# Products over token chunks of 458, 458 and 254 columns, with one 508-column matmul for the high and low parts of the last chunk

## What is computed

```python
D_MODEL, D_FF, CONV_W = 1024, 2816, 3

def conv_ffn(x, left, g, w_gate, w_up, cw, cb, w_down):
    xn = rms_norm(x, g)
    a = xn @ w_gate
    L = x.shape[1]
    ap = jnp.concatenate([left.astype(a.dtype), a], axis=1)
    ac = cb + sum(ap[:, j:j + L] * cw[j] for j in range(CONV_W))
    y = (jax.nn.gelu(ac) * (xn @ w_up)) @ w_down
    return y, ap[:, -(CONV_W - 1):]

# in each of the two layers: x = x + attention(rms_norm(x) @ w_in) @ w_o; x = x + conv_ffn(x, ...)
```

## Time and profile before

| | us |
|---|---|
| median of 3 runs | 3441.87 |
| lowest, highest | 3436.18, 3450.18 |
| the profiled execution | 3446.24 |
| its span from first to last instruction | 3444.3 |
| PE busy in it | 3284.8 |
| DVE, ACT, POOL busy | 1624.4, 781.4, 881.8 |

### The profile page before, as it was taken

One profiled execution on the slowest core, in us unless ns is written; L12 is line 12 of the kernel. 1 busy time (PEld: TensorE's weight loads), 2 busy tenths in 40 slices (PEclk: granted clock), 3 DMA queues, 4 the chain that ended last, 5 costly groups with the idle time before them and its releaser, 6 DMA issues.

```text
span 3444.3 us, 49534 instructions
## 1 busy us (share of the span) xinstructions
PE 3284.8 (95%) x17911; PEld 3017.1 (88%) x17911; DVE 1624.4 (47%) x3150; ACT 781.4 (23%) x1867; POOL 881.8 (26%) x943
## 2 busy tenths in 40 slices
PE   8979999999999999999985999999999999999998
PEld 7957778899999999987684777777989999999997
DVE  4033442454444454454697355544244444444445
ACT  3043553100000000032454335443210000000001
POOL 3211222322222222231132133221232222222321
PEclk9955999999999999999996569999999999999998
DMA  3520000111111111122111000000211111111111
GB/s 106 82 75 1 1 2 19 37 37 43 37 43 43 37 42 37 39 83 50 23 48 46 21 1 1 1 1 1 76 36 44 43 37 43 43 37 37 43 43 64
DMA packets 179634, 129.18 MB, mean 38 GB/s; under 512 B 30961, under 2 KB 169649, under 8 KB 179270
## 3 DMA queue, kind: packets, MB, share of 16 engines
q1 hardware_dynamic: 179490, 127.32, 12.9%
HBM read 111.62 MB, written 15.16 MB: 37 GB/s over the span
## 4 chain that ended last, share of the span: by engine, by line
PE 88%; DVE 6%; issue 4%; ACT 1%; SPq 1%; DMA 0%; DVEq 0%; POOL 0%; POOLq 0%; ACTq 0%
PE ps_gemm L1235 30%; PE ps_gemm L1251 16%; PE ps_gemm L1201 14%; PE ps_out L1583 7%; PE ps_out L1417 5%; PE ps_tr L1301 4%; PE ps_far L1563 2%; PE ps_far L1465 2%; PE ps_near L1565 2%; PE ps_far L1397 1%; PE ps_tr L1287 1%; DVE xl L1821 1%; DVE pta L1816 1%; DVE m L2049 1%; DVE pt_b L1816 1%
## 5 line engine op out<-in xcount | busy, mean ns | idle before, releaser
L569 DVE TENSOR_TENSOR h<-h,ps_gemm 128x1170 f32<-128x1170 f32 x192 | 263.7, 1373 | 409.1 <-PE ps_gemm L1251 231.5
L1235 PE MATMUL ps_gemm<-xh,w_hi 128*128 128x390 f32 x1920 | 448.1, 341 | 0.0
L1235 PE MATMUL ps_gemm<-xh,w_lo 128*128 128x390 f32 x1920 | 448.1, 342 | 0.0
L1235 PE MATMUL ps_gemm<-xl,w_hi 128*128 128x390 f32 x1920 | 446.1, 340 | 0.0
L1077 POOL CAST w_hi<-w_raw 128x1024 fp32r<-128x1024 f32 x120 | 125.1, 1042 | 1129.1 <-PE ps_gemm L1235 623.8
L1235 PEld LDWEIGHTS ps_gemm<-xh,w_hi 128*128 128x128 f32 x1920 | 352.5, 189 | 0.0
L1235 PEld LDWEIGHTS ps_gemm<-xl,w_hi 128*128 128x128 f32 x1920 | 349.4, 189 | 0.0
L1235 PEld LDWEIGHTS ps_gemm<-xh,w_lo 128*128 128x128 f32 x1920 | 349.1, 189 | 0.0
L1080 POOL TENSOR_TENSOR w_lo<-w_raw,w_hi 128x1024 fp32r<-128x1024 f32 x120 | 288.2, 2402 | 18.5 <-POOL w_hi L1077 2.5
L1201 PE MATMUL ps_gemm<-xl,w_hi 128*128 128x390 f32 (+1 forms) x1152 | 275.3, 348 | 0.0
L1251 PE MATMUL ps_gemm<-gu_hi,w_hi 128*128 128x390 f32 x1056 | 247.4, 342 | 1.0 <-DVE h L569 1.0
(11 more groups left out here) (287 smaller groups left out, 5304.4 us busy)
## 6 DMA issues: line engine op xcount, KB each, us to landing
w_raw<-in_w_gate SPq DMA_DIRECT2D x44, 512.0 KB, 3.8
w_raw<-in_w_up SPq DMA_DIRECT2D x44, 512.0 KB, 3.8
w_raw<-in_w_down SPq DMA_DIRECT2D x44, 512.0 KB, 3.2
w_raw<-in_w_in_b SPq DMA_DIRECT2D x13, 512.0 KB, 4.3
w_raw<-in_w_qkv_a SPq DMA_DIRECT2D x10, 512.0 KB, 3.9
residual_park<-h SPq DMA_DIRECT2D x1, 4680.0 KB, 13.7
h<-residual_park SPq DMA_DIRECT2D x8, 585.0 KB, 8.7
out<-yt SPq DMA_DIRECT2D x9, 512.0 KB
```

Source lines behind the costliest of these rows:

```text
L569: dve.tensor_tensor(c3(h[:, m, :]), c3(h[:, m, :]), pse(j), ALU.add).then_inc(evac[j % 2], 1)
L1235: mm = pe.matmul(ps[j % 2][:, m_, 0:CH], w[:, k, :], x[:, k, m_ * CH:(m_ + 1) * CH], start=(k == 0 and w is wh and x is XH), stop=(k == KT ...
```

## The change

The chunks become 458, 458 and 254 columns (CH = 458, WL = 254). XH and XL become two halves of one tensor XX, gu_hi and gu_lo two halves of GU. In the FFN (`split=True`) the product of a high weight block with the third chunk of the high part and that of the low part become one matmul over 2 x 254 = 508 columns, which leaves the high part's sum in columns 0 to 253 of the third bank and the low part's in columns 254 to 507; so a block has eight matmuls there. VectorE adds the two halves: `tail_copy` copies the second half to a tile, `tail_of` adds the first half to it, and the consumer reads the tile. Outside the FFN (`split=False`) a block keeps nine matmuls, three of them of 254 columns. All takers of PSUM now use one instruction for the two chunks of 458 and one for the last chunk. The RMS scale is computed over the new chunks.

```diff
-CH = T // NCH
+CH = 458
+CHUNKS = ((0, CH), (CH, 2 * CH), (2 * CH, T))
+WL = T - 2 * CH
...
+        def bank_pair(j, r=slice(0, P)):
+
+            return ps[j % 2][r, 0:2, 0:CH]
+
+        def bank_last(j, r=slice(0, P)):
+
+            return ps[j % 2][r, 2, 0:WL]
+
+        def bank_rest(j, r=slice(0, P)):
+
+            return ps[j % 2][r, 2, WL:2 * WL]
...
+        def tail_copy(dve, j):
+
+            dve.tensor_copy(tail[j % 2][:], bank_rest(j)).then_inc(tail_in, 1)
+
+        def tail_of(dve, j, i=None):
+
+            wait_at(dve, tail_in, 2 * tail_no(j) + 1, 24, i)
+            dve.tensor_tensor(tail[j % 2][:], bank_last(j), tail[j % 2][:], ALU.add).then_inc(tail_in, 1)
+            wait_at(dve, tail_in, 2 * tail_no(j) + 2, 24, i)
+            return tail[j % 2][:]
...
-        def residual(dve, j, m, i=None):
+        def residual(dve, j, m, i=None, merged=True):
 
             wait_at(dve, mm_done, j + 1, 12, i)
-            dve.tensor_tensor(c3(h[:, m, :]), c3(h[:, m, :]), pse(j), ALU.add).then_inc(evac[j % 2], 1)
+            src = bank_last(j)
+            if merged:
+                tail_copy(dve, j)
+            dve.tensor_tensor(cols_pair(h[:, m, :]), cols_pair(h[:, m, :]), bank_pair(j), ALU.add)
+            if merged:
+                src = tail_of(dve, j, i)
+            dve.tensor_tensor(cols_last(h[:, m, :]), cols_last(h[:, m, :]), src, ALU.add).then_inc(evac[j % 2], 1)
...
+                tail_copy(dve, j)
                 dve.tensor_tensor(ga[:, 2:2 + 2 * CH].rearrange("p (c n) -> p c n", c=2), src[:, 0:2, 0:CH],
                                   R[:, 0:2 * CH].rearrange("p (c n) -> p c n", c=2), ALU.mult)
...
+                last = tail_of(dve, j, i)
...
-                dve.tensor_tensor(c3(gb[:]), pse(j), c3(R[:]), ALU.mult).then_inc(evac[j % 2], 1)
+                tail_copy(dve, j)
+                dve.tensor_tensor(cols_pair(gb), bank_pair(j), cols_pair(R), ALU.mult)
+                dve.tensor_tensor(cols_last(gb), tail_of(dve, j, i), cols_last(R), ALU.mult).then_inc(evac[j % 2], 1)
...
+            def products(bank, wh, wl, xh, xl, x_both, n, first, last, split):
+
+                pe.matmul(bank[0:n, 0, 0:CH], wh, xh[:, 0:CH], start=first, stop=False)
+                pe.matmul(bank[0:n, 1, 0:CH], wh, xh[:, CH:2 * CH], start=first, stop=False)
+                both = bank[0:n, 2, 0:2 * WL].rearrange("p (a n) -> p a n", a=2)
+                if split and not last:
+                    pe.matmul(both, wh, x_both, start=first, stop=False)
+                elif not split:
+                    pe.matmul(bank[0:n, 2, 0:WL], wh, xh[:, 2 * CH:T], start=first, stop=False)
+                    pe.matmul(bank[0:n, 2, 0:WL], wh, xl[:, 2 * CH:T], start=False, stop=False)
+                pe.matmul(bank[0:n, 0, 0:CH], wh, xl[:, 0:CH], start=False, stop=False)
+                pe.matmul(bank[0:n, 1, 0:CH], wh, xl[:, CH:2 * CH], start=False, stop=False)
+                pe.matmul(bank[0:n, 0, 0:CH], wl, xh[:, 0:CH], start=False, stop=last)
+                pe.matmul(bank[0:n, 1, 0:CH], wl, xh[:, CH:2 * CH], start=False, stop=last)
+                mm = pe.matmul(bank[0:n, 2, 0:WL], wl, xh[:, 2 * CH:T], start=False, stop=last and not split)
+                if split and last:
+                    mm = pe.matmul(both, wh, x_both, start=False, stop=True)
+                return mm
...
-                    for w, x in ((wh, x_hi), (wh, x_lo), (wl, x_hi)):
-                        for m in range(NCH):
-                            mm = pe.matmul(ps[j % 2][0:n, m, 0:CH], w[:, k, 0:n], x[:, k, m * CH:(m + 1) * CH],
-                                           start=(k == 0 and w is wh and x is x_hi), stop=(k == KT - 1 and w is wl))
+                    mm = products(ps[j % 2], wh[:, k, 0:n], wl[:, k, 0:n], x_hi[:, k, :], x_lo[:, k, :],
+                                  XX[:, 0:2, k, 2 * CH:T], n, k == 0, k == KT - 1, split)
...
-                        residual(dve, j0 + k, k)
+                        residual(dve, j0 + k, k, None, m not in (1, 3))
```

More of the change, by code:

```diff
@@ L503, in build @@
         conv_step = sem("conv_step")
+        tail_in = sem("last_columns_added")
+        tail = [x4["tail0"], x4["tail1"]]
         gel_done = sem("gelu_done")
@@ L580, in tile @@
                     wait_at(act, mm_done, jd, 12, i)
-                copy(x3["gu_hi"][:, u, :], x4["gb"][:]).then_inc(guh_done, 1)
+                copy(GU[:, 0, u, :], x4["gb"][:]).then_inc(guh_done, 1)
             F0 = l * FT
@@ L1188, in tr_free, with gemm @@
                     pe.wait_ge(tr_out[g % 2], g // 2)
-            def gemm(c, j, x_hi, x_lo, n=P, gate=None):
+            def products(bank, wh, wl, xh, xl, x_both, n, first, last, split):
[15 more added lines that the diff above has]
+                return mm
+            def gemm(c, j, x_hi, x_lo, n=P, gate=None, split=False):
                 pe.wait_ge(w_split, c + 1)
@@ L1210, in square_sum @@
                 pe.wait_ge(tr_out[1], g // 2)
-                for i in range(NCH):
+                for i, (c0, c1) in enumerate(CHUNKS):
                     if i == 2:
                         pe.wait_ge(ss_out, 3 * m + 1)
-                    pe.matmul(tb[i % 2][:, 0:CH], mean_w[:], x4["acc"][:, i * CH:(i + 1) * CH],
+                    pe.matmul(tb[i % 2][:, 0:c1 - c0], mean_w[:], x4["acc"][:, c0:c1],
                               start=True, stop=True).then_inc(ss_done, 1)
             def ffn(c0, j0, m, gu0, g_ctx):
-                guh, gul = x3["gu_hi"], x3["gu_lo"]
-                gemm(c0, j0, XH, XL, gate=8 * m)
+                gemm(c0, j0, XH, XL, gate=8 * m, split=True)
                 square_sum(m, G_END_A if m == 1 else G_END_B)
                 for k in range(1, 4):
-                    gemm(c0 + k, j0 + k, XH, XL)
+                    gemm(c0 + k, j0 + k, XH, XL, split=True)
                 def job(c, j, i, n_it):
@@ L1232, in job @@
                     for k in range(KT):
-                        for w, x in ((wh, XH), (wh, XL), (wl, XH)):
-                            for m_ in range(NCH):
-                                mm = pe.matmul(ps[j % 2][:, m_, 0:CH], w[:, k, :], x[:, k, m_ * CH:(m_ + 1) * CH],
-                                               start=(k == 0 and w is wh and x is XH), stop=(k == KT - 1 and w is wl))
+                        mm = products(ps[j % 2], wh[:, k, :], wl[:, k, :], XH[:, k, :], XL[:, k, :],
+                                      XX[:, 0:2, k, 2 * CH:T], P, k == 0, k == KT - 1, True)
                     mm.then_inc(mm_done, 1)
@@ L1248, in down @@
                             wh, wl = whi[(c + u) % 3], wlo[(c + u) % 3]
-                            for w, x in ((wh, guh), (wh, gul), (wl, guh)):
-                                for i_ in range(NCH):
-                                    mm = pe.matmul(ps[(j + m_) % 2][:, i_, 0:CH], w[:, m_, :], x[:, u, i_ * CH:(i_ + 1) * CH],
-                                                   start=(u == 0 and w is wh and x is guh), stop=(u == 1 and w is wl))
+                            mm = products(ps[(j + m_) % 2], wh[:, m_, :], wl[:, m_, :], GU[:, 0, u, :], GU[:, 1, u, :],
+                                          GU[:, 0:2, u, 2 * CH:T], P, u == 0, u == 1, True)
                         mm.then_inc(mm_done, 1)
@@ L1672, in norm @@
                     act.activation(dst[:], h[:, k, :], ACT.Square).then_inc(sq_done, 1)
-                for i in range(NCH if m < 4 else 0):
+                for i, (c0, c1) in enumerate(CHUNKS if m < 4 else ()):
                     act.wait_ge(ss_done, 3 * m + i + 1)
-                    act.activation(R[:, i * CH:(i + 1) * CH], tb[i % 2][:, 0:CH], ACT.Sqrt, bias=eps[:, 0:1]).then_inc(ss_out, 1)
+                    act.activation(R[:, c0:c1], tb[i % 2][:, 0:c1 - c0], ACT.Sqrt, bias=eps[:, 0:1]).then_inc(ss_out, 1)
             def attention(units, steps, x_of, w_of, op, out_lo, pt, pt_w, unit0, pair0, pre):
@@ L1779, in take_projection @@
                 if i == 5:
[L1780 to L1782 removed]
+                    copy(cols_pair(x4["kt2"]), bank_pair(j))
+                    copy(cols_last(x4["kt2"]), bank_last(j)).then_inc(evac[j % 2], 1)
+                else:
+                    copy(cols_pair(q[:, i - 6, :]), bank_pair(j), -HD ** -0.5)
+                    copy(cols_last(q[:, i - 6, :]), bank_last(j), -HD ** -0.5).then_inc(evac[j % 2], 1)
             def take_kv_b(g):
@@ L1831, in scale @@
             def scale(m):
-                for i in range(NCH):
+                for i, (c0, c1) in enumerate(CHUNKS):
                     dve.wait_ge(ss_out, 3 * m + i + 1)
-                    r = R[:, i * CH:(i + 1) * CH]
+                    r = R[:, c0:c1]
                     dve.reciprocal(r, r).then_inc(r_done, 1)
```

56 lines of the change are left out of this document (33 added, 23 removed).

## The result

The changed kernel takes 3468.73 us (median of 7 runs, 3459.36 to 3481.68), the kernel before on the same chip 3439.59 (7 runs, 3429.89 to 3450.18). The ratio is 1.0087, 95% interval 1.0063 to 1.0112: slower by 0.9%. A ratio is that of the fast executions alone and leaves out those that took over 1.5% longer than the fastest of the same kernel, so further down it can differ from that of the medians. The profiled execution of the changed kernel took 3481.68 us, its span is 3480.1.

What follows compares the result with a forecast made beforehand. PE was taken to bound the kernel, alone in the FFN loop. A 17.4 us saving against added VectorE costs summed to +2.1 us: 3448.3 for the profiled execution, median about 3444, range 3420 to 3478.

Steps and rivals of the forecast that it cites:

- rival 3: Down jobs' first slots: VectorE's residual longer than 2.21 us, each 0.1 costing 8 us; at 2.5, 3468 us; chance 0.16.
- TensorE, 1056 matmuls fewer: FFN blocks of both layers: eight matmuls instead of nine, each saving a fixed 16.5 ns, 17.4 us in all.
- residuals in the down jobs: FFN loop: longer merged residuals overfill VectorE's first slots, stalling PE 0.54 us a round, +10.8 us over 20 rounds.
- gate and up in the loop: FFN loop: 0.9 us extra evacuation work, up to 3, hidden under 5 us of cover; costs nothing.
- layer 0's end, with its last up: Behind layer 0's loop VectorE is the bound: residuals delay banks, +5.0 us; last ups cost +1.8 for both layers.
- layer 1's end, with its last up: Layer 1's end: only the last residual shows, +0.9 us; last ups cost +1.8 for both layers.
- two-instruction takes elsewhere: Other PSUM takes: 0.06 to 0.2 us more each, mostly hidden under 12.9 us jobs; +1.0 us (0 to 3).
- its 0.66 us: Down jobs in the loop: slack between a merged residual freeing its bank and PE needing it one slot later.
- The price of a matmul: FFN float32r matmuls: 16.6 ns above 162.5 read as fixed per matmul; the other reading, per column, saves nothing.
- rival 1: FFN matmuls: the extra goes with columns, merge saves nothing, gate or up job 12.89 us; +16.3, 3458 us; chance 0.17.
- the second rival: All float32r matmuls: a floor of 179 ns whatever the width, streaming hidden beneath; -4.5, 3437 us; chance 0.11.
- Rivals 2 and 4: 254-column matmuls: floor of 179 ns (3437 us, chance 0.11), or half rate, 215 instead of 122 ns (3619 us, 0.10).

Runs made afterwards that it cites:

- e7: Changed kernel, but GpSimd splits the next up weights behind the fifth down job instead of right behind gate: 3469.75 us, ratio 1.008.
- e6: Changed kernel with the merge only in the down jobs; gate and up keep nine matmuls a block, taken directly from PSUM: 3460.93 us, ratio 1.0029.
- e8: Changed kernel with GpSimd's split behind the fifth down job, bank release in the loop after adding the halves, each layer's last eight down jobs unmerged: 3437.57 us, ratio 0.9969.
- e10: Changed kernel, residuals adding both halves from PSUM, split behind fifth down job, last eight down jobs unmerged; run twice: 3439.28 us (ratio 0.9948), 3389.41 us (0.9847).
- e4: Changed kernel, but in the FFN loop GpSimd splits the next weights only once VectorE has taken out the job's bank: 3468.22 us, ratio 1.0088.

## Why the prediction was right and wrong

The likeliest case was no difference, 3444; it came out 0.9% slower, 3468.7. That is inside the range (3420 to 3478), at the price of rival 3 (3468), and outside the forecast's own range (3433 to 3456). The range held because it was wide enough for the rivals; the forecast's mechanism does not lead to this time. The terms:

| term | forecast | measured |
|---|---|---|
| TensorE, 1056 matmuls fewer | -17.4 | -8.4 |
| residuals in the down jobs | +10.8 | +6.2 |
| gate and up in the loop | 0 | +24.6 |
| layer 0's end, with its last up | +5.9 | +6.2 |
| layer 1's end, with its last up | +1.8 | +3.3 |
| two-instruction takes elsewhere | +1.0 | +0.3 (2.0) |
| sum | +2.1 | +32.2 |

The measured terms stand against +30.0 at equal clock and +29.1 between the medians. The 2 to 3 us between them are not accounted for; each end is read from one execution and holds 0.2 us of TensorE's gain, which the first row counts too. The loop's two terms are 20 times those of a round. At gate the late job starts 1.39 us behind the matmul ahead of it (1053.01 to 1054.40), 1.16 over the usual 0.23, and 0.07 go to the restart: 1.23. At the sixth down job 0.24 and 0.07 make 0.31.

**The step that failed** is "gate and up in the loop: nothing, 5 us of cover". The 5 us were those of up's chain, between its end at 1040.40 and the down jobs that read its result from 1045.45 on the earlier trace rows. Gate's evacuation has another reader waiting: the bank, which TensorE wants one down job later, 3.2 us after gate ended. The prediction used just this slack for the residuals (its 0.66 us) and did not ask for it at gate, which uses the same two buffers. Even so gate would have made it: without the collision it needs 2.4 us (e7, where L651 takes 0.29). The stretch, "up to 3 if GpSimd's split slows the two-SBUF-operand adds", was named and sized well enough, 1.6 us at L651, but was laid against the wrong cover. That rows of the kernel before showed the same collision was missed as well. This group of it was not among those read: the product of up with the convolution's result, both in SBUF.

```profile
L648 DVE TENSOR_TENSOR gb<-gb,ac 128x1040 f32<-128x1040 f32 x44 | 133.8, 3040 | 9.9 <-DVE gb L644 9.8
```

In the round of the earlier trace rows it ran beside GpSimd's subtraction, and ended at 1037.39, behind that one's 1036.28:

```profile
1034.29 3.10 DVE L648 TENSOR_TENSOR gb<-gb,ac 128x1040 f32<-128x1040 f32 x1 [0.24 <-DVE gb L644]
...
1033.88 2.40 POOL L1080 TENSOR_TENSOR w_lo<-w_raw,w_hi 128x1024 fp32r<-128x1024 f32 x1
```

In the changed kernel the same instruction is L690 and takes 1.24 us, since the product L686 ahead of it now meets the split:

```profile
L686 DVE TENSOR_TENSOR gb<-tail,rms_scale 128x254 f32<-128x254 f32 x44 | 86.3, 1961 | 4.3
...
L651 DVE TENSOR_TENSOR ga<-tail,rms_scale 128x124 f32<-128x124 f32 x44 | 79.9, 1816 | 4.3
L690 DVE TENSOR_TENSOR gb<-gb,ac 128x1040 f32<-128x1040 f32 x44 | 54.7, 1242 | 9.9 <-DVE gb L686 9.8
```

The collision had been in the kernel all along, in up's chain, where 5 us cover it. The merge brought an SBUF operand into gate's chain, where they don't.

**The price of a matmul** was the second step mis-sized: 16.5 ns fixed was taken, 8 ns came back. Both readings of the prediction were half right. With 3510 columns in each, a block of eight takes 1603.5 ns and one of nine with 458 and 254 columns 1612.5 (output projections, 12.90 us a job), so a matmul has a fixed price of 9 ns and a column 0.436; the nine equal matmuls of before (1611.6) give 8 and 0.438. The starts themselves, averaged over layer 0's loop, lie 118, 209 and 231 ns behind 254, 458 and 508 columns; a line through the first two has 5 ns and 0.447 and gives 232 for the third. So the 8 ns of a block are sure, how they and the rest divide into the two parts is known to a few ns, and that the 508 columns come from two places costs nothing that shows. A gate or up job lasts 12.83 us, between the 12.76 of the forecast and the 12.89 of rival 1.

**The residuals' stall** was right in mechanism and nearly in size. They take 2.2 us as worked out from the earlier trace rows (1054.18 to 1056.38 in the changed kernel), and where nothing else holds TensorE up they cost 0.76 (e6) or 0.67 us (e7) against 0.54. What the sum left out is mainly 0.07 us at each restart. In the changed kernel itself the term is smaller, since TensorE's wait at gate gives the residuals time.

**Layer 0's end** came out as forecast, +6.2 for +5.9, and it is the residuals of the last down jobs: unmerged there, it falls back (73.2 and 73.5 in e8 and e10), with the shorter adds it is 75.7. The sign that the prediction gave for it, a longer wait before the last job, did not come (0.20 us, where it was 0.65): TensorE waits 1.40 us before the fifth job, 2.30 before the seventh and 2.24 before the projection behind, where it had waited 0, 0.31 and 0.42 us. The chain is not quite the forecast's either, for L607 is stretched here too, by GpSimd's additions of squares. These had stretched the low parts before (L1821 at 3.31, 2.89 and 2.89 us, 1.43 without them), which now run in their usual time, so the collision changed its place, 4.8 us of it before and 3.9 after, and that the total came out so close is in part luck. Two of the stretched adds, and the wait before the seventh job:

```profile
1532.23 2.36 DVE L607 TENSOR_TENSOR h<-h,tail 128x254 f32<-128x254 f32 x1
...
1542.43 1.39 DVE L607 TENSOR_TENSOR h<-h,tail 128x254 f32<-128x254 f32 x1
...
1543.97 0.44 PE L1234 MATMUL ps_gemm<-gu,w_hi 128*128 128x458 f32 x1 [2.30 <-DVE h L607]
```

Layer 1's end has the same stretch (L607 at 1.15 to 1.50 us beside three of GpSimd's additions) and was 1.5 above forecast; 1.6 of its 3.3 us (2.2 in the second profile) stay in the last version, with the down jobs unmerged, and were not followed further.

**Of the rivals,** rival 3 had the right sign and total. Its mechanism was right in its bracket (two SBUF operands beside GpSimd) and wrong in its place: residuals in the loop did not grow, gate's evacuation did, so that its total came out is luck. Its sign, waits over 1.5 us a round, came too (1.56) and would have misled. Rival 1 holds for half of the price of a matmul or more. A saving of 2.6 us, which the prediction sets near the second rival (3437), would make its sum +16.9 us or 3459, and that is near the first (3458). Rivals 2 and 4 fall: 254 columns start 0.12 us apart, neither 0.18 nor 0.21.

## What to carry to other kernels

Ask of every evacuation which of its results is wanted first: the value it computes or the buffer it reads; the cover is the smaller of the two, and a long cover for the one says nothing of the other. When a change makes VectorE read from SBUF what it read from PSUM, look for what GpSimd does at that time, and look in the trace of before for an instruction with both operands in SBUF whose mean is far above its size. Work that saves TensorE a matmul is worth its fixed price only (here 8 us in 3440), so it pays only if what it adds elsewhere fits every single slot; here the loop kept the gain once the halves were added straight from PSUM and the split was moved, though the whole kernel shows it only at equal clock.

## What the runs showed of the hardware

VectorE's instruction with two SBUF operands that came up during GpSimd's subtraction of 128 x 1024 ended behind it by its own usual time less some 0.14 us, as if it began only there: L651 (124 columns, 0.29 us by itself) at 1054.05 for 1053.91, L607 (254 columns, 0.42) at 1055.29 for 1055.01 in e7 and at 1064.35 for 1064.07 in e4, L648 of the kernel before (1040 columns, 1.24) at 1037.39 for 1036.28. So the price on top of its own time is what is left of GpSimd's 2.4 us when it comes up, whatever its size. GpSimd's subtraction took 2.39 to 2.41 us with or without it. In the other order GpSimd paid: its addition of squares that began at 1559.30, during VectorE's L1877 (1559.08 to 1560.51, also two SBUF operands), took 3.79 us, where those that began ahead of VectorE's took 2.67 to 2.69. The Trainium skill (SBUF — State Buffer, "Who interferes with whom") has this as a rule: an instruction of VectorE with two inputs in SBUF shares a read port with GpSimd's reads, the later of the two is blocked until the other is through, and one SBUF input at most does not contend. The traces here agree on each point, with L359, L604 and L611 (one operand in PSUM, 0.41, 1.10 and 0.41 us beside the split) for the last.

A float32r matmul at the full clock costs 5 to 9 ns plus 0.436 to 0.447 ns a column, from 254 to 508 columns, if the price is made of these two parts (8 to 9 by the blocks, 5 by the mean starts), and 508 columns that come from two places in memory cost no more than their number. The Trainium skill (TensorE: Matmul & The Clock Gate, "Back-to-back issue gap") has 2.5 ns and N / 2.4 for an isolated matmul; both parts are larger here, by the measured blocks and by the starts.
